# A two-block transformer kernel: the mLSTM cells' products evenly spaced, column sums four steps later, the third mixer's round reordered

## Chip, core, metric

One NeuronCore of a Trainium2 chip runs one program. The metric is device time in microseconds (us); lower is better.

## What is computed

The reference is a float32 model of two blocks on 512 positions of width 1024. The first block (Fourier and latent attention mixers, gated convolutional FFN) is not touched. The second has two layers, each a mixer, a squared-ReLU FFN and a gated embedding. The mixers, cut to what matters here:

```
# mixer_ab: two chains, 4 heads of 128, chunks of 64 positions (8 chunks)
qa, ka = l2norm(silu(conv(..))), l2norm(silu(conv(..)))     # gated delta rule, chain A
v_new = u - w @ state;  o = q_dec @ state + attn @ v_new    # per chunk
state = state * exp(g_last) + k_dec.T @ v_new
# mLSTM, chain B, per chunk
num = inter * (q @ c_st) + pmat @ v                         # numerators
den = inter * (q @ n_st) + sum(pmat)
c_st = sc * c_st + kw.T @ v;  n_st = sc * n_st + sum(kw)
out = concat(rmsnorm(oa)*silu(z), rmsnorm(num/max(|den|,..))*o_gate) @ w_out
# mixer_c: 16 heads of 64, 4 key/value heads, window 128
q, k = rope(q), rope(k)
sc = q @ k.T * 64**-0.5  (band mask);  m = max(max(sc), sink)
pr = exp(sc - m) / (sum(exp(sc - m)) + exp(sink - m));  o = pr @ v
out = o @ w_o + b_o
```

## The kernel before

Every big product goes through `linear`. It walks "weight units" of 1024 x 128 in one global stream. A unit is 8 k-tiles; for each k-tile TensorE issues three 128x128 by 128x512 matmuls (high weight by high input, high by low, low by high; L393). ScalarE and VectorE split each unit into its high and low parts (L340, L349), three units ahead. Units of one `linear` alternate between PSUM banks 0 and 1 in the mixers; ScalarE empties a bank when its unit is done. The first two units of a `linear` run interleaved.

The mixers' small products are woven between those matmuls. Each engine has a chain written as a generator, with `until(name, n)` before each piece; after every second k-tile TensorE calls `tick(pe, 2)`, which lets its chain go on to the next two clock values. So one hook stands after each six matmuls of 512 columns, four hooks and eight ticks in a unit. ScalarE and VectorE advance by eight ticks at once, ahead of their wait for that unit's end; a piece of theirs that waits for TensorE therefore holds up the emptying of the unit behind it. No planner orders anything: the numbers in `until` do. With two generators on an engine (chain and side) each gets every tick.

`mixer_ab` (`chain_ab`) weaves both chains into the 33 units of the input projection. `unit_columns` (L1809) sums squares of a head over its 128 rows by 4 products of one column; it needs ScalarE's `norm_squares` (L2037). `unit_spread` (L1818) spreads the reciprocal roots; `apply` multiplies by them. The delta rule's cells follow (L1924 to L1938), then the mLSTM's eight cells. A cell has a first part (state increments L1983, intra-chunk numerators L1989 and denominators L1991) and, for n > 0, a second part with the carried state (L1997, L1999), which waits for VectorE's state update (L2239). In the program the 128x129 and 64-column products have four heads each. `mix_out` is the output projection: its input tiles 0 to 3 come from chain A (`fin["a"]`), 4 to 7 from chain B, and are split by ScalarE (L2376) and VectorE (L2383).

`mixer_c` (`chain_c`) weaves attention into 12 units, one pair of query heads t per round of eight ticks (`begin = 33 + 8t`), the last ones into `mix_out`. A round on TensorE: `swap` (L2483, half-rotation for rope), `turn` (L2490, 8 transposes of probabilities, twice), scores (L2520, 16 rows of the trace), values (L2537, 32 rows). VectorE does rope (L2577, L2580), mask (L2589), row maximum (L2591, L2593), `divide` (L2598, L2600), the copy of bank 7 (L2606) and the low part of the result (L2648). ScalarE does exp (L2545), the copy of bank 6 (L2552), the high part (L2563), and empties the projection's banks (L2470, `put`). GpSimd does the cosine product (L2683) and the division (L2689). Bank 2 is shared by `swap` and scores, bank 3 by scores and values. At the start VectorE computes the angles in ten dependent steps (L2617 to L2625), then ScalarE two Sin (L2556, L2557).

Of the kernel before, what the change touches and what calls it, by code (L numbers as in the profile page):

```python
# [14 lines left out]
P = 128  # L15
# [353 lines left out]
def linear(c, args, x, kt, count, n, ready, free, scalar=None, vector=None, scalar2=None, vector2=None, width=None,  # L369
           group=2, fill=None, before=None, supply=None, weave=None, slots=3, tick=None, third=0):  # L370
# [4 lines left out]
    cols = lambda j: width(j) if width else n  # L375
    block = c.stage()

    @block.tensor
    def _(pe):
# [8 lines left out]
        def products(j, k):  # L388
            p = pos + j
            w = slice((p % WSLOTS) * UN + k * P, (p % WSLOTS) * UN + k * P + P)  # L390
            for z, (wt, xt) in enumerate(((c.WHI, xh), (c.WHI, xl), (c.WLO, xh))):
                for acc, lo, q in accumulator(c, p, cols(j), slots):
                    mm = pe.matmul(acc, wt[:, w], xt[:, k * xw + lo:k * xw + lo + q],  # L393
                                   start=(k == 0 and z == 0), stop=(k == kt - 1 and z == 2))
            if k == kt - 1:
                mm.then_inc(c.units_done, 1)
# [3 lines left out]
        for k in range(kt):  # L400
# [11 lines left out]
        for j in range(group, count):  # L412
# [5 lines left out]
            for k in range(first, kt):  # L418
# [1205 lines left out]
def chain_ab(c, args, xp, ready, before, fin):  # L1624
# [52 lines left out]
    clock = {"pe": 0, "act": 0, "dve": 0}  # L1677

# [143 lines left out]
    def pe_chain(pe):  # L1822
# [8 lines left out]
        for h in range(4):  # L1831
            yield from until("pe", 44 + 8 * h)
            unit_columns(pe, stat["K"], o["SQK"], h)
        for h in range(4):
            yield from until("pe", 71 + h)
# [132 lines left out]
        for n in range(NCH):  # L1968
            yield from until("pe", 200 + 3 * n)
# [23 lines left out]
            if n:  # L1993
                yield
# [6 lines left out]
        for h in range(4):  # L2001
            yield from until("pe", 226 + h)
            unit_columns(pe, b_stat, o["SQ"], h)
        for h in range(4):
            yield from until("pe", 233 + h)
            unit_spread(pe, b_stat, 7, h, 2 + h)

    def pe_side(pe):
        for h in range(4):
            yield from until("pe", 76 + 8 * h)  # L2010
            unit_columns(pe, stat["Q"], o["VB"], h)
        for h in range(4):
            yield from until("pe", 103 + h)
# [25 lines left out]
    def act_chain(act):  # L2039
# [4 lines left out]
        yield from until("act", 69)  # L2044
# [52 lines left out]
        for n in range(NCH):  # L2097
            yield from until("act", 202 + 3 * n)
# [3 lines left out]
        for h in range(4):  # L2102
            yield from until("act", 225 + h)
# [3 lines left out]
        yield from until("act", 231)  # L2107
# [3 lines left out]
    def act_side(act):  # L2111
# [4 lines left out]
        yield from until("act", 101)  # L2116
# [19 lines left out]
    def dve_chain(dve):  # L2136
        id4 = c.a(o["ID2"], CHUNK).rearrange("p (a q) -> p a q", a=1).broadcast_to([P, 4, CHUNK])
        lasts = lambda lo: c.a(o["LAST"] + lo, NCH).rearrange("p (n a) -> p n a", a=1)
        yield from until("dve", 70)
        dve.wait_ge(*stat["K"][2].at(1))  # L2140
        dve.reciprocal(root(1), root(0)).then_inc(*stat["K"][3].up())
        for h in range(4):
            yield from until("dve", 71 + h)
# [84 lines left out]
        for n in range(NCH - 1):  # L2228
            yield from until("dve", 201 + 3 * n)
# [14 lines left out]
        yield from until("dve", 226)  # L2244
# [8 lines left out]
        yield from until("dve", 231)  # L2253
# [7 lines left out]
        for h in range(4):  # L2261
            yield from until("dve", 233 + h)
# [4 lines left out]
    def dve_side(dve):  # L2267
        lasts = lambda lo: c.a(o["LAST"] + lo, NCH).rearrange("p (n a) -> p n a", a=1)
        yield from until("dve", 102)
        dve.wait_ge(*stat["Q"][2].at(1))  # L2270
        dve.reciprocal(root(3), root(2)).then_inc(*stat["Q"][3].up())
        for h in range(4):
            yield from until("dve", 103 + h)
# [83 lines left out]
def mixer_ab(c, args, squares):  # L2357
# [7 lines left out]
    with c.pair(NL) as xp:  # L2365
        xh, xl, xw = xp
        hi, lo = c.mark("act", KT), c.mark("dve", KT)
        source = lambda k: c.a(A2["OA"] + k * NL, NL) if k < 4 else c.a(A2["QB"] + (k - 4) * NL, NL)
        block = c.stage()

        @block.scalar
        def _(act):
            act.wait_ge(c.units_done, c.pos)
            for k in range(KT):
# [4 lines left out]
        def _(dve):  # L2379
            for k in range(KT):  # L2380
                dve.wait_ge(*hi.at(k + 1))
                q = slice(k * xw, k * xw + NL)
                dve.tensor_tensor(xl[:, q], source(k), xh[:, q].bitcast(F32), ALU.subtract).then_inc(*lo.up())  # L2383
        squares = mix_out(c, args, xp, lambda k: lo.at(k + 1), c.h)
# [51 lines left out]
def chain_c(c, args, xp, ready, xh, xl):  # L2436
# [55 lines left out]

    def pe_chain(pe):
# [10 lines left out]
        for t in range(9):  # L2504
            begin = 33 + 8 * t
            yield from steps.until("pe", begin)
            if t < 8:
                swap(pe, 2 + t)
            if t:
                yield from steps.until("pe", begin + 1)  # L2510
                turn(pe, 2 * t - 2)
            if t < 8:
                yield from steps.until("pe", begin + 2)
                own(pe, (2, 3), masked.at(2 * t + 1))
                own(pe, (4, 5), masked.at(2 * t + 2))
                pe.wait_ge(*roped.at(3 + t))
                for j in range(4):
                    for r in range(2):
                        q = (64 * r, 64 * r + 64)
                        mm = pe.matmul(c.bank(2 + 2 * r + j // 2, 256, (j % 2) * 256), c.a(o["Q"] + t * NL + j * P, P, *q),  # L2520
                                       c.a(o["K"] + (t // 4) * (NL + P) + j * P, 2 * WIN, *q), start=True, stop=True)
                mm.then_inc(*scores.up())
            if t:
                yield from steps.until("pe", begin + 4)
                turn(pe, 2 * t - 1)
                yield from steps.until("pe", begin + (6 if t < 7 else 4))
                own(pe, (3,), low.at(t))
                pe.wait_ge(*pt_a.at(2 * t))
                pe.wait_ge(*pt_v.at(2 * t))
                if t == 1:  # L2530
                    pe.wait_ge(*v_put.at(2))
                    pe.wait_ge(*cleared.at(3))
                for j in range(4):
                    for z in range(2):
                        for r in range(2):
                            kv = 2 * ((t - 1) // 4) + r
                            mm = pe.matmul(c.bank(3, P, j * P, 64 * r, 64 * r + 64), c.a(o["V"] + (j + z) * 256 + kv * 64, 64),  # L2537
                                           pt(r, (2 * j + z) * P, P), start=(z == 0), stop=(z == 1))
                mm.then_inc(*values.up())
# [14 lines left out]
    def act_chain(act):  # L2554
        act.wait_ge(*angle.at(10))
        act.activation(sin, tmp(1), ACT.Sin).then_inc(*wave.up())  # L2556
        act.activation(cos, s(0, NL, NL), ACT.Sin).then_inc(*wave.up())  # L2557
        for t in range(10):
            begin = 33 + 8 * t
            yield from steps.until("act", begin)  # L2560
            if t >= 2:
                act.wait_ge(*values.at(t - 1))
                act.activation(xh[:, (t - 2) * NL:(t - 1) * NL], c.bank(3), ACT.Copy).then_inc(*high.up())  # L2563
            if 1 <= t <= 8:
                exp(act, 2 * t - 1)
                copy_a(act, 2 * t - 2)
                yield from steps.until("act", begin + 3)
                copy_a(act, 2 * t - 1)
            if t < 8:
                yield from steps.until("act", begin + 4)  # L2570
                exp(act, 2 * t)
# [634 lines left out]
```

## Time and profile before

| | us |
|---|---|
| median of 3 runs | 3305.43 (3297.83 to 3309.86) |
| the profiled execution, its own time | 3311.63 |
| its span | 3309.8 |
| TensorE busy | 3179.3 |
| VectorE busy | 1560.5 |
| ScalarE busy | 1164.3 |
| GpSimd busy | 166.5 |

In the trace mixer_ab with its output projection stands at about 1800 to 2236 us and mixer_c at about 2675 to 2880 us. A matmul row counts as busy whatever the clock, so TensorE's busy time hides half-clock stretches; the granted clock (1.00 is 2.4 GHz, 0.50 is 1.2 GHz) is in a column of its own. A float32 product written once in the program makes two rows in the trace.

### The profile page before, as it was taken

How to read it: one execution, taken by the hardware profiler on the slowest of the kernel's cores; microseconds unless marked ns; L12 is line 12 of the kernel's file. 1: busy time of each engine (PE TensorE's matmuls, PEld its weight loads, DVE VectorE, ACT ScalarE, POOL GpSimd, SP SyncE). 2: the span in 40 equal slices, each digit the busy share in tenths (PEclk: the TensorE clock that was granted, in tenths of full speed). 3: DMA queues.
4: the chain of work that ended last, by engine and by line, in shares of the span. 5: the costliest groups of instructions: out<-in, count | busy, mean ns of one | idle time of the engine just before them, and what ended most of it. 6: DMA issues, size and time to landing. Idle time of an engine off the chain costs nothing.

```text
span 3309.8 us, 42475 instructions
## 1 busy us (share of the span) xinstructions
PE 3179.3 (96%) x17484; PEld 2511.5 (76%) x17484; DVE 1560.5 (47%) x2346; ACT 1164.3 (35%) x1892; POOL 166.5 (5%) x222
## 2 busy tenths in 40 slices
PE   7999999999999999999999999999999988899999
PEld 4656687888888756788887777877888767788887
DVE  3234544434445445564557453236334567453445
ACT  3134523213223334442334532234222435332233
POOL 0022200000000012000000010000000014000000
PEclk9999999999999999999998899799999999999999
DMA  7500014333212300122322111023222221222222
GB/s 278 215 1 1 7 45 159 120 132 124 64 58 77 118 2 1 52 94 97 96 96 81 54 32 44 32 70 102 90 95 96 77 75 38 76 96 96 96 96 70
DMA packets 74031, 269.28 MB, mean 81 GB/s; under 512 B 9064, under 2 KB 9832, under 8 KB 72560
## 3 DMA queue, kind: packets, MB, share of 16 engines
q1 hardware_dynamic: 73840, 266.57, 23.7%
q8 instruction: 140, 2.29, 0.3%
q14 instruction: 51, 0.42, 0.0%
HBM read 264.44 MB, written 2.10 MB: 81 GB/s over the span
## 4 chain that ended last, share of the span: by engine, by line
PE 87%; DVE 5%; issue 3%; ACT 2%; DMA 1%; POOL 1%; SPq 0%; DVEq 0%; POOLq 0%; ACTq 0%
PE PS L393 65%; PE PS L1366 4%; PE PS L1389 2%; PE PS L1376 2%; PE PS L1292 2%; PE PS L486 1%; DMA room<-in_w_ada 1%; PE PS L1346 1%; POOL room L2689 1%; PE PS L2947 1%; PE PS L570 0%; DVE room L1716 0%; PE PS L1320 0%; PE PS L1809 0%; PE PS L1818 0%
## 5 line engine op out<-in xcount | busy, mean ns | idle before, releaser
L393 PE MATMUL PS<-room,WHI 128*128 128x512 f32 (+1 forms) x7200 | 2030.9, 378 | 31.6 <-ACT room L2470 6.2
L393 PEld LDWEIGHTS PS<-room,WHI 128*128 128x128 f32 x7200 | 1264.1, 190 | 325.5 <-issue 61.4
L393 PE MATMUL PS<-room,WLO 128*128 128x512 f32 (+1 forms) x3600 | 1242.7, 375 | 0.0
L393 PEld LDWEIGHTS PS<-room,WLO 128*128 128x128 f32 x3600 | 636.1, 190 | 125.2
L349 DVE TENSOR_TENSOR WLO<-RING,WHI 128x1024 fp32r<-128x1024 f32 x371 | 455.1, 1227 | 278.8 <-ACT WHI L340 277.4
L340 ACT ACTIVATE WHI<-RING 128x1024 fp32r<-128x1024 f32 x371 | 390.3, 1054 | 557.4 <-PE PS L393 523.8
L931 DVE SCALAR_TENSOR_TENSOR H<-PS,VEC,H 128x511 f32<-128x511 f32 (+1 forms) x132 | 83.1, 657 | 307.3 <-ACT H L909 307.3
L909 ACT ACTIVATE H<-PS,VEC 128x512 f32<-128x512 f32 (+1 forms) x132 | 88.4, 704 | 348.8 <-PE PS L393 348.8
L1366 PE MATMUL PS<-room 96*128 96x256 f32 (+1 forms) x432 | 155.8, 480 | 10.4 <-DVE room L1528 8.1
L874 DVE SCALAR_TENSOR_TENSOR X<-PS,MOD,X 128x512 f32<-128x512 f32 x96 | 60.5, 658 | 217.4 <-PE PS L393 217.4
L1572 DVE TENSOR_REDUCE room<-PS 128x1 f32<-128x768 f32 (+1 forms) x120 | 101.9, 849 | 98.9 <-PE PS L1366 98.4
L1366 PEld LDWEIGHTS PS<-room 96*128 96x128 f32 x432 | 74.7, 191 | 64.7 <-issue 57.3
L2990 DVE TENSOR_TENSOR room<-PS,room 128x512 f32<-128x512 f32 x64 | 44.2, 690 | 165.8 <-ACT room L2986 107.5
L2986 ACT ACTIVATE room<-PS 128x512 f32<-128x512 f32 x64 | 38.1, 596 | 199.1 <-PE PS L393 199.1
L1592 POOL TENSOR_SCALAR room<-room 128x768 f32<-128x768 f32 (+1 forms) x60 | 49.2, 820 | 1135.6 <-DVE room L1558 1135.6
L3015 DVE TENSOR_TENSOR X<-X,PS 128x512 f32<-128x512 f32 x48 | 33.0, 687 | 134.2 <-PE PS L393 134.2
L1552 DVE COPY room<-PS 128x384 f32<-128x384 f32 (+1 forms) x120 | 59.5, 496 | 59.2 <-PE PS L1376 59.0
L936 DVE SCALAR_TENSOR_TENSOR H<-PS,VEC,H 128x511 f32<-128x511 f32 (+1 forms) x132 | 83.2, 658 | 3.1
L486 PE MATMUL PS<-room,SC 128*32 128x512 f32 x336 | 59.5, 738 | 25.9 <-DMA room<-in_w_ada 25.9
L1389 PE MATMUL PS<-room 128*64 128x128 f32 x1248 | 82.7, 280 | 1.2 <-DVE room L1552 1.2
L1389 PEld LDWEIGHTS PS<-room 128*64 128x64 f32 x1248 | 68.1, 138 | 20.5 <-issue 18.9
L1292 PE MATMUL PS<-room 128*128 128x512 f32 (+1 forms) x210 | 77.3, 514 | 0.0
(370 smaller groups left out, 2622.8 us busy)
## 6 DMA issues: line engine op xcount, KB each, us to landing
RING<-in_stream SPq DMA_DIRECT2D x370, 512.0 KB, 3.4
room<-in_w_ada SPq DMA_DIRECT2D x84, 512.0 KB, 5.7
H<-in_w_ada SPq DMA_DIRECT2D x12, 512.0 KB, 4.6
room<-in_consts SPq DMA_DIRECT2D x4, 1024.0 KB, 9.2
room<-in_wq SPq DMA_DIRECT2D x2, 1728.0 KB, 6.9
X<-in_x_in SPq DMA_DIRECT2D x2, 1536.0 KB, 10.0
room<-in_wple SPq DMA_DIRECT2D x2, 1024.0 KB, 4.9
out_dram<-H SPq DMA_DIRECT2D x8, 256.0 KB, 2.0
```

What stands on the lines that cost most here:

```text
L340: act.activation(c.WHI[:, w:w + UN], c.RING[:, r:r + UN], ACT.Copy).then_inc(c.w_hi, 1)
L349: dve.tensor_tensor(c.WLO[:, w:w + UN], c.RING[:, r:r + UN], c.WHI[:, w:w + UN].bitcast(F32), ALU.subtract).then_inc(c.w_lo, 1)
L393: mm = pe.matmul(acc, wt[:, w], xt[:, k * xw + lo:k * xw + lo + q], start=(k == 0 and z == 0), stop=(k == kt - 1 and z == 2))
L486: mm = pe.matmul(c.bank(self.bank, 512, 0, 32 * j, 32 * j + 32), c.SC[:, 32 * k:32 * k + 32], self.ring[self.slots[k]][j // 2][:, 512 * (j ...
L909: ins = act.activation(cv(i, z, lo, w), a, ACT.Identity, bias=col("b_dw", j), scale=col("dw1_", j))
L931: ins = dve.scalar_tensor_tensor(y, a[:, 0:w - 1], col("dw0_", j), y, ALU.mult, ALU.add)
L936: ins = dve.scalar_tensor_tensor(y, a[:, 1:w], col("dw2_", j), y, ALU.mult, ALU.add)
L1292: mm = pe.matmul(c.bank(b + r, m), c.a(w + k * stride, P), c.a(x + k * W + lo, m), start=(k == 0), stop=(k == kn - 1))
L1366: mm = pe.matmul(c.bank(b + r, m), q_at(p, z, i * P, P, 0, 96), k_at(p, z, k0 + lo, m, 0, 96), start=True, stop=True)
L1376: mm = pe.transpose(c.bank(4 + (k >= half), P, (k % half) * P), probs_at(a, k * P, P), c.ID[:])
L1389: mm = pe.matmul(c.bank(6 + part, P, (i % 4) * P, 64 * z, 64 * z + 64), c.a(vv + (t0 + t) * 768 + (2 * pair + z) * 64, 64), turned_at(a + ...
L1572: dve.tensor_reduce(c.a(NEG + j, 1), c.PS[:, 512 * b:512 * b + n], AX, ALU.max, negate=True).then_inc(*neg.up())
```

## The change

1. **mLSTM cells.** `cell_at(n) = 198 + 4n` (200 for n = 0) replaces `200 + 3n`. The second part comes two ticks after the first, for every cell; before, one tick, which was in the same hook for every second cell. Their followers (column sums, roots, spreads and products at the end of chain B) move 4 to 10 ticks later. Chain A's spreads at the end stay.
2. **Column sums later.** Those of K go from ticks 44 + 8h to 48 + 8h, those of Q from 76 + 8h to 80 + 8h, with roots and spreads four ticks later. ScalarE's squares and the blocks after them stay.
3. **mix_out of mixer_ab** takes input tiles 4 to 7 first, then 0 to 3; the splitting follows.
4. **mixer_c.** ScalarE's Sin and VectorE's use of it move to tick 9, after the first two units' emptying. In a round the values of head pair t-2 are taken beside `swap`; the scores of t come two k-tiles later than before, ahead of `turn(2t-2)`; `turn(2t-1)` is in the last hook. ScalarE's exp of a pair all goes into the next round, ahead of its copies; VectorE's mask is parted from its maximum (`peak`), with a copy in between; GpSimd divides pair t-1 in one go after its cosine product. No instruction is added or removed on TensorE.

```diff
-           group=2, fill=None, before=None, supply=None, weave=None, slots=3, tick=None, third=0):
+           group=2, fill=None, before=None, supply=None, weave=None, slots=3, tick=None, third=0, order=None):
+    ks = order or list(range(kt))
-        for k in range(kt):
+        for k in ks:
...
+    cell_at = lambda n: 198 + 4 * n if n else 200
...
-            yield from until("pe", 44 + 8 * h)
+            yield from until("pe", 48 + 8 * h)
             unit_columns(pe, stat["K"], o["SQK"], h)
...
-            yield from until("pe", 200 + 3 * n)
+            yield from until("pe", cell_at(n))
...
             if n:
-                yield
+                yield from until("pe", cell_at(n) + 2)
...
-            yield from until("pe", 226 + h)
+            yield from until("pe", 234 + h)
             unit_columns(pe, b_stat, o["SQ"], h)
...
-            yield from until("pe", 233 + h)
+            yield from until("pe", 243 + h)
...
-            yield from until("pe", 76 + 8 * h)
+            yield from until("pe", 80 + 8 * h)
             unit_columns(pe, stat["Q"], o["VB"], h)
...
-            yield from until("act", 202 + 3 * n)
+            yield from until("act", cell_at(n) + (3 if n else 1))
...
-            yield from until("dve", 201 + 3 * n)
+            yield from until("dve", cell_at(n) + 1)
...
+        order = [4, 5, 6, 7, 0, 1, 2, 3]
...
+            if 2 <= t < 8:
+                take_values(pe, t - 2)
+            if t < 8:
+                yield from steps.until("pe", begin + (4 if t < 7 else 1))
+                score(pe, t)
             if t:
-                yield from steps.until("pe", begin + 1)
                 turn(pe, 2 * t - 2)
...
-                yield from steps.until("pe", begin + 4)
+                yield from steps.until("pe", begin + (6 if t < 7 else 4))
                 turn(pe, 2 * t - 1)
...
+            if t >= 7:
+                take_values(pe, t - 1)
...
     def act_chain(act):
+        yield from steps.until("act", 9)
         act.wait_ge(*angle.at(10))
...
+            if 1 <= t <= 8:
+                exp(act, 2 * t - 2)
...
-            if t < 8:
-                yield from steps.until("act", begin + 4)
-                exp(act, 2 * t)
```

**Order on TensorE, the mLSTM cells.** Before, a first part with its second part, six matmuls of 512 columns (L393), and the next cell's first part:

```order
L1983 MATMUL PS<-room 128x129 x4
L1989 MATMUL PS<-room 128x64 x4
L1991 MATMUL PS<-ONES,room 64x1 x4
L1997 MATMUL PS<-X,room 128x64 x4
L1999 MATMUL PS<-room,X 64x1 x4
L393 MATMUL PS<-room,WHI 128x512 x2
L393 MATMUL PS<-room,WLO 128x512
L393 MATMUL PS<-room,WHI 128x512 x2
L393 MATMUL PS<-room,WLO 128x512
L1983 MATMUL PS<-room 128x129 x4
```

Now (lines shifted by two, L393 is L394):

```order
L1985 MATMUL PS<-room 128x129 x4
L1991 MATMUL PS<-room 128x64 x4
L1993 MATMUL PS<-ONES,room 64x1 x4
L394 MATMUL PS<-room,WHI 128x512 x2
L394 MATMUL PS<-room,WLO 128x512
L394 MATMUL PS<-room,WHI 128x512 x2
L394 MATMUL PS<-room,WLO 128x512
L1999 MATMUL PS<-X,room 128x64 x4
L2001 MATMUL PS<-room,X 64x1 x4
```

Three of the seven cells with a second part had both parts in one hook before; now every part has six matmuls of 512 columns on either side.

**Order on VectorE, one attention round.** Before, from rope to the weight split:

```order
L2577 TENSOR_TENSOR room<-PS,room 128x512
L2580 TENSOR_TENSOR room<-H,room 128x512
L2648 TENSOR_TENSOR room<-PS,room 128x512
L2606 COPY room<-PS 128x512
L2598 TENSOR_TENSOR MS<-MS 128x4
L2600 RECIPROCAL MS<-MS 128x4
L2589 SCALAR_TENSOR_TENSOR room<-PS,room 128x1024
L2591 TENSOR_REDUCE MS<-room 128x4
```

Now (L2586 and L2589 rope, L2609 and L2611 `divide`, L2662 the low part, L2598 mask, L2617 the copy, L2602 the maximum):

```order
L2586 TENSOR_TENSOR room<-PS,room 128x512
L2589 TENSOR_TENSOR room<-H,room 128x512
L2609 TENSOR_TENSOR MS<-MS 128x4
L2611 RECIPROCAL MS<-MS 128x4
L2662 TENSOR_TENSOR room<-PS,room 128x512
L2609 TENSOR_TENSOR MS<-MS 128x4
L2611 RECIPROCAL MS<-MS 128x4
L2598 SCALAR_TENSOR_TENSOR room<-PS,room 128x1024
L2617 COPY room<-PS 128x512
L2602 TENSOR_REDUCE MS<-room 128x4
```

Both divides now stand between rope and the mask, and the copies stand behind the masks.

## Rows read from the trace of the kernel before

**Rows 1.** The page, its first line and part 1.
```profile
span 3309.8 us, 42475 instructions
...
PE 3179.3 (96%) x17484; PEld 2511.5 (76%) x17484; DVE 1560.5 (47%) x2346; ACT 1164.3 (35%) x1892; POOL 166.5 (5%) x222
```

**Rows 2.** Waits of TensorE, 1825 to 2200 us: total, times, longest.
```profile
PE PS L1809 <- ACT room L2037: 9.6, 5, 3.2
PE PS L393 <- DVE room L2383: 2.3, 1, 2.3
PE PS L1818 <- DVE room L2260: 2.1, 1, 2.1
```

**Rows 3.** Timeline, 1830 to 1840 us: start, duration, instruction, idle before.
```profile
1836.91 0.61 ACT L2037 ACTIVATE room<-room 128x512 f32<-128x512 f32 x1
...
1837.67 1.84 PE L1809 MATMUL PS<-ONES,room 128*128 128x1 f32 x8 [3.15 <-ACT room L2037]
```

**Rows 4.** Busy time by engine in four stretches, then TensorE's granted clock.
```profile
1825.00:1915.00 90.00, 79.48 (x484) 61.85 (x482) 39.20 (x71) 45.02 (x81) 3.17 (x5) 0.85 0.13 45
2003.00:2050.00 47.00, 47.00 (x297) 37.97 (x295) 16.44 (x35) 8.46 (x14) 0.00 (x0) 1.00 0.11 35
2089.40:2103.00 13.60, 13.60 (x107) 11.91 (x106) 4.43 (x14) 3.21 (x5) 0.00 (x0) 1.00 0.12 40
2103.00:2151.40 48.40, 48.40 (x220) 40.97 (x218) 6.62 (x18) 3.46 (x7) 0.00 (x0) 0.54 0.07 22
```

**Rows 5.** Timeline of TensorE, 2097 to 2104 us.
```profile
2097.44 1.00 PE L1997 MATMUL PS<-X,room 128*128 128x64 f32 x8
...
2098.93 0.74 PE L393 MATMUL PS<-room,WHI 128*128 128x512 f32 x2
...
2100.53 1.16 PE L1983 MATMUL PS<-room 64*128 64x129 f32 x8
...
2103.01 1.37 PE L1997 MATMUL PS<-X,room 128*128 128x64 f32 x8
```

**Rows 6.** Groups by line and form, TensorE, 2103 to 2151.4 us.
```profile
L393 PE MATMUL PS<-room,WLO 128*128 128x512 f32 x14 | 8.8, 628 | 0.0
L1997 PE MATMUL PS<-X,room 128*128 128x64 f32 x40 | 8.0, 370 | 0.0
L1983 PE MATMUL PS<-room 64*128 64x129 f32 x32 | 7.7, 412 | 0.0
```

**Rows 7.** Waits of TensorE, 2680 to 2845 us.
```profile
PE PS L2520 <- DVE room L2648: 7.9, 5, 1.6
PE PS L393 <- ACT room L2470: 6.2, 2, 5.9
PE PS L2490 <- POOL room L2689: 3.4, 2, 3.0
PE PS L393 <- DVE room L2648: 2.9, 2, 1.4
PE PS L2520 <- DVE room L2580: 2.1, 2, 1.1
PE PS L2537 <- DVE room L2606: 1.8, 2, 0.9
PE PS L2483 <- ACT room L2470: 1.5, 1, 1.5
```

**Rows 8.** Busy time and clock, start of mixer_c and five attention rounds.
```profile
2690.00:2701.00 11.00, 8.46 (x23) 6.14 (x24) 6.68 (x10) 4.20 (x6) 3.34 (x2) 0.69 0.32 97
2745.86:2816.06 70.20, 63.63 (x453) 50.21 (x454) 50.63 (x80) 36.91 (x114) 29.92 (x45) 1.00 0.12 39
```

**Rows 9.** Timeline of ScalarE, 2690 us.
```profile
2690.76 0.63 ACT L2556 ACTIVATE room<-room 128x512 f32<-128x512 f32 x1 [5.60 <-DVE room L2625]
```

**Rows 10.** Timeline of GpSimd, 2740 us.
```profile
2740.20 2.88 POOL L2689 TENSOR_SCALAR room<-room,MS 128x256 f32<-128x256 f32 x4 [5.72 <-DVE MS L2600]
```

**Rows 11.** The page, part 5, weight splitting on VectorE.
```profile
L349 DVE TENSOR_TENSOR WLO<-RING,WHI 128x1024 fp32r<-128x1024 f32 x371 | 455.1, 1227 | 278.8 <-ACT WHI L340 277.4
```

More of the change, by code:

```diff
@@ L417, in _ @@
                 begin(j)
-            for k in range(first, kt):
+            for k in ks[first:]:
                 products(j, k)
@@ L2102, in act_chain @@
         for h in range(4):
-            yield from until("act", 225 + h)
+            yield from until("act", 231 + h)
             if h == 0:
@@ L2106, in act_chain @@
             norm_squares(act, b_stat, "QB", h, o["SQ"])
-        yield from until("act", 231)
+        yield from until("act", 237)
         act.wait_ge(*m_den.at(5))
@@ L2261, in dve_chain @@
         for h in range(4):
-            yield from until("dve", 233 + h)
+            yield from until("dve", 241 + h)
             if h == 0:
@@ L2373, in _ @@
             act.wait_ge(c.units_done, c.pos)
-            for k in range(KT):
+            for k in order:
                 act.wait_ge(*(fin["a"].at(k + 1) if k < 4 else fin["b"].at(k - 3)))
@@ L2379, in _ @@
         def _(dve):
-            for k in range(KT):
-                dve.wait_ge(*hi.at(k + 1))
+            for i, k in enumerate(order):
+                dve.wait_ge(*hi.at(i + 1))
                 q = slice(k * xw, k * xw + NL)
                 dve.tensor_tensor(xl[:, q], source(k), xh[:, q].bitcast(F32), ALU.subtract).then_inc(*lo.up())
-        squares = mix_out(c, args, xp, lambda k: lo.at(k + 1), c.h)
+        squares = mix_out(c, args, xp, lambda k: lo.at(order.index(k) + 1), c.h, order=order)
     c.high = None
@@ L2491, in turn, with score, take_values @@
         mm.then_inc(*turned.up())
+    def score(pe, t):
+        own(pe, (2, 3), masked.at(2 * t + 1))
+        own(pe, (4, 5), masked.at(2 * t + 2))
+        pe.wait_ge(*roped.at(3 + t))
+        for j in range(4):
+            for r in range(2):
+                q = (64 * r, 64 * r + 64)
+                mm = pe.matmul(c.bank(2 + 2 * r + j // 2, 256, (j % 2) * 256), c.a(o["Q"] + t * NL + j * P, P, *q),
+                               c.a(o["K"] + (t // 4) * (NL + P) + j * P, 2 * WIN, *q), start=True, stop=True)
+        mm.then_inc(*scores.up())
+    def take_values(pe, v):
+        own(pe, (3,), low.at(v + 1))
+        pe.wait_ge(*pt_a.at(2 * v + 2))
+        pe.wait_ge(*pt_v.at(2 * v + 2))
+        if v == 0:
+            pe.wait_ge(*v_put.at(2))
+            pe.wait_ge(*cleared.at(3))
+        for j in range(4):
+            for z in range(2):
+                for r in range(2):
+                    kv = 2 * (v // 4) + r
+                    mm = pe.matmul(c.bank(3, P, j * P, 64 * r, 64 * r + 64), c.a(o["V"] + (j + z) * 256 + kv * 64, 64),
+                                   pt(r, (2 * j + z) * P, P), start=(z == 0), stop=(z == 1))
+        mm.then_inc(*values.up())
     def pe_chain(pe):
@@ L2628, in dve_chain @@
         dve.memset(c.a(o["V"], 256), 0.0).then_inc(*cleared.up())
+        yield from steps.until("dve", 9)
         dve.wait_ge(*wave.at(2))
@@ L2674, in _ @@
     def _(pool):
-        for t in range(-2, 9):
-            i = t + 2
+        for i in range(11):
             if i < 10:
```

78 lines of the change are left out of this document (27 added, 51 removed).

## The prediction

> **What bounds the kernel now.** I read the page first. TensorE is busy 3179.3 of 3309.8 us [rows 1], so a gain can come from two places only: the 130 us in which TensorE stands still, and stretches in which it works at a lower clock, which its busy time doesn't show. The page's slices of granted clock dip around 2100 us, so I asked for the busy time by stretch there, then for TensorE's waits in the two mixers that the change touches, and last for the timeline around each wait.
>
> In mixer_ab, the waits between 1825 and 2200 us are led by the column sums: 9.6 us in five waits for ScalarE's squares, then 2.1 us for a reciprocal before the second chain's spreads and 2.3 us at the start of mix_out [rows 2]. Worse than these is the clock. From 2103.0 to 2151.4 us, TensorE is "busy" 48.4 of 48.4 us at a mean clock of 0.54 [rows 4], so it works at 1.2 GHz for nearly the whole stretch, without standing still once. These are the mLSTM cells. The delta rule's cells, woven with one part in each hook, kept 1.00 throughout (2003 to 2050 us) [rows 4]. In mixer_c the waits sum to 25.8 us [rows 7]: 7.9 for the low part of the values in five rounds, 5.9 once at the start, the rest at the first two rounds and the end.
>
> **The change part by part, as a sum.**
>
> *(a) Second part apart from the first.* What stands right before the fall: a second part (2097.44), six wide matmuls (2098.93), a first part (2100.53) and, at 2103.01, a second part with nothing wide between [rows 5]. From there each instruction takes longer: a product of L1997 rows 1.37 against 1.00 us for eight. Pieces at full clock, from start to start: second part 1.49, six wide matmuls 1.60, first part 2.48 us. The slow stretch holds 14 low-part matmuls, so 7 packs of six, 40 rows of L1997, so 5 second parts, and 32 rows of L1983, so 4 first parts [rows 6]. At full clock that is 5 x 1.49 + 4 x 2.48 + 7 x 1.60 = 28.6 us, against 48.4 measured: 19.8 us. The new order never joins two parts, and its densest stretch of small products is the first part alone, 2.48 us between two packs. In the 13.6 us before the fall, two first parts stood alone like this and the clock was 1.00 [rows 4]. I take the whole 19.8; the other end is zero, since nothing in the trace shows eight cells in the new spacing. The state update has time: a second part now comes two packs and a part behind the increments that it waits for.
>
> The Trainium skill ("TensorE: Matmul & The Clock Gate", section "Why this matters for your kernels") has the clock fall when TensorE stands idle between bursts of matmuls. Here it fell with no idle time at all, so the trace says more than that rule; by the rule alone spacing the parts would change nothing, which is the second case below.
>
> *(b) Sums four ticks later.* A sum now has 12 wide matmuls more ahead of it, 2 x 1.60 = 3.2 us at full clock. The longest of the five waits is 3.2 us [rows 2]: the squares start at 1836.91 and the sum at 1837.67 after 3.15 us idle [rows 3]. All five are covered, 9.6 us. For Q each square also moves ahead of the sum by a whole unit of ScalarE's queue, since the squares stay at their ticks. What is queued behind: reciprocal, spreads and `apply` move too, and ScalarE now waits for the first turned K tile one hook into the next unit before it may empty the last one. That bank isn't needed for another unit, over 5 us; I put 0.6 us against it. The mean clock over 1825 to 1915 us is 0.85 [rows 4]: 0.15 x 90 / 0.5 = 27 us at half clock. The clock falls at the four-column products before the first sum, which stay, and around the waits. I let half of the 27 us go; 3 of these 13.5 us are the first wait itself, so 10.5 us of work at half clock become 5.2. Bounds 0 and 10. Sum of (b): 9.6 - 0.6 + 5.2 = 14.2 us.
>
> *(c) End of chain B.* The spreads come ten ticks later, over a unit of wide matmuls, and the reciprocal is there: 2.1 us. The new order of input tiles in mix_out is worth nothing by itself: the first low part (L2383) stands on VectorE behind the last tile of chain A, whichever tile it makes, so the 2.3 us stay [rows 2].
>
> *(d) Start of mixer_c.* ScalarE held the finished first units back while it waited for the angles: 5.60 us, then Sin at 2690.76 [rows 9], and the emptying only behind it. Now it empties first, and the third unit starts at once. But the angles are no earlier, so Sin still ends near 2692. VectorE first splits two weight units at 1.23 us each [rows 11] and only then rotates, so the first rotation is read out at about 2695.2. TensorE reaches the second `swap`, which needs the same bank, after 18 wide matmuls (3 x 1.60) from 2686.7, so near 2691.8, and waits some 3.4 us. Of 5.9 us 2.5 go. The clock there is 0.69 over 11 us [rows 8], 6.8 us at half; half of the loss goes, 1.7. Sum 4.2 us; bounds 1 and 8.
>
> *(e) First two attention rounds.* Gone: 1.5 for a bank's emptying (exp no longer stands ahead of it), 2.1 for rope, since scores come one hook later, 0.4 of the 3.4 for GpSimd [rows 7]. Together 4.0; 3.5 after what may stay.
>
> *(f) Five full rounds.* Now 70.2 / 5 = 14.04 us each, with 7.9 us of waits in all [rows 7, 8], so 12.46 us of work. I follow a new round from its unit's start: swap and values at 1.5, scores 6.7 to 8.6, first turn to 9.4, second turn at 10.9. VectorE, after scores: mask, copy, maximum, mask, copy, maximum, split, until about 16.8, then rope until 18.1. TensorE wants the next scores at 6.7 + 12.4 = 19.1: 1 us of room. VectorE has 50.6 / 5 = 10.1 us of work in a round, GpSimd 6.0 [rows 8]; neither fills 12.4. GpSimd's division takes up to 2.88 us [rows 10] from about 18.5, so it ends by 21.4, and the first turn comes at 21.1: a wait of a few tenths at worst. I leave 0.2 us a round: 7.9 - 1.0 = 6.9 us; bounds 0 and 9.
>
> *(g) End of mixer_c.* There 8.0 us stand now: 3.0 for GpSimd, 2.9 for low parts, 1.8 for copies, 0.3 for a bank [rows 7]. The last pair still runs alone through exp, division, turn, copy, values and split; following the new queues the same way leaves 6.6. Gain 1.4.
>
> Sum: 19.8 + 14.2 + 2.1 + 4.2 + 3.5 + 6.9 + 1.4 = 52.1 us. The profiled execution took 3311.63, which gives 3259.5. It lies 6.2 us above the median of the runs, 3305.43; taken from that, 3253.3. I say **3254**.
>
> **The other ways it could go.**
>
> *The clock falls in the cells anyway.* For it: a part and its neighbour are still small products for over half the time, and the parts of the delta rule that kept 1.00 have no one-column products. Against: the fall came just at the joined parts [rows 5]. Then the 19.8 us stay: 3274. Chance 0.20.
>
> *Attention becomes bound by its helpers.* VectorE now has nearly everything between one round's scores and the next's in one string; 1 us of room is little, and if rope, GpSimd's cosine or the division come 1.5 us late, TensorE waits at the scores or the turn instead. Then (f) and part of (e) give nothing: 3254 + 9 = 3263. Chance 0.12; with the case above, 3283, 0.03.
>
> *Slower.* The half clock starts at the first cell and isn't shaken off, because packs of six don't suffice to raise it. All cells then run at the ratio of 48.4 to 28.6, 1.7: 8 first and 7 second parts with 15 packs are 19.8 + 10.4 + 24.0 = 54 us at full clock, 92 at half. The same work took 13.7 + 48.4 + about 4.6 = 67 us before: 25 us more. Should the remaining 35 us up to mix_out stay slow too, another 25. Less (b) to (g), 32.3, that is 18 us slower, 3323. It decides only if the slow clock outlasts the cells. Chance 0.03.
>
> *The change does little.* If each removed wait comes back one instruction later, as (d) partly shows, and the clock falls too, the time stays within 0.5%, which is about what a measurement of this kernel can tell from no change. Chance 0.05.
>
> **How the numbers follow.** The forecast's own case has 0.57. Faster by over 0.5% (below 3289) are it and the two next ones with their joint case, 0.92; within 0.5%, 0.05; slower 0.03. For the range: upward, the clock's case at 3274 and the joint one at 3283 go in. Downward, the high ends of (b), (d) and (f) with 0.5 us of waits gone elsewhere give 10 us or so: 3242. I say 3240 to 3284.
>
> **What the profile will show.** (a): granted clock of 1.00 across the cells, L1985 rows never followed by L1999 rows. (b): no wait of the sums for ScalarE, five before. (c): no wait for the reciprocal, still 2.3 us at mix_out's start. (d): a wait of some 3.4 us at the second `swap`, none at the third unit. (f): rounds of 12.4 to 12.8 us without a wait before scores. The prediction is wrong if the clock in the cells is below 1.00 for more than 10 us, or if rounds still take 14 us.

## The result: 39 us faster, 13 us short of the sum

The changed kernel took 3265.96 us (median of 4 runs, 3263.37 to 3275.56) against 3305.35 before (4 runs, 3297.83 to 3309.86): ratio 0.9884, 95% interval 0.9862 to 0.9906. It is faster, inside the range and 12 us above the 3254 that were forecast: it gains 39.4 us where the sum has 52.1. The execution of it that was profiled took 3275.56, so the two profiles lie 36.0 us apart (spans 3309.8 and 3273.8 us).

The page of the changed kernel, first line and part 1:

```profile
span 3273.8 us, 42474 instructions
PE 3160.7 (97%) x17484; PEld 2495.8 (76%) x17484; DVE 1560.0 (48%) x2346; ACT 1164.7 (36%) x1891; POOL 159.8 (5%) x222
```

TensorE's busy time fell by 18.6 us with the same products [rows 1]: about half of the distance between the profiles is clock, the other half waits. Its waits in the two mixers, first 1825 to 2200 us, against [rows 2]:

```profile
PE PS L394 <- DVE room L2386: 2.3, 1, 2.3
PE PS L1820 <- DVE room L2143: 2.2, 1, 2.2
PE PS L2032 <- ACT room L1732: 1.4, 1, 1.4
PE PS L1843 <- DVE H L2151: 1.0, 1, 1.0
...
PE PS L1848 <- DVE room L2158: 0.4, 1, 0.4
PE PS L1887 <- ACT room L2065: 0.3, 1, 0.3
PE PS L1811 <- ACT room L2039: 0.3, 1, 0.3
```

The 9.6 us of the column sums (L1811 now) are down to 0.3, but the first K spread (L1820) now waits 2.2 us for its reciprocal (L2143) and two steps behind it 1.4 us together. Then 2620 to 2830 us, against [rows 7]:

```profile
PE PS L2486 <- DVE room L2586: 4.9, 1, 4.9
PE PS L394 <- DVE room L2662: 2.8, 2, 1.4
PE PS L2503 <- DVE room L2589: 2.4, 1, 2.4
PE PS L2518 <- DVE room L2617: 1.7, 2, 0.9
...
PE PS L394 <- ACT room L2473: 1.4, 1, 1.4
PE PS L2493 <- POOL room L2701: 1.2, 1, 1.2
```

Low part (L394 for L2662) and copy (L2518 for L2617) of the last pair stay; the second `swap` (L2486) waits 4.9 us and the second scores (L2503) 2.4. The full rounds up to the scores at 2768.65 us have no wait; the 1.4 us for a bank stand right behind them, at 2775.35. The rows of the second `swap` and of the scores, TensorE, 2673 to 2769 us:

```profile
2673.89 1.73 PE L2486 MATMUL PS<-room,MS 128*128 128x512 f32 x2 [4.95 <-DVE room L2586]
...
2705.80 2.00 PE L2503 MATMUL PS<-room 64*128 64x256 f32 x16 [2.39 <-DVE room L2589]
...
2718.53 2.00 PE L2503 MATMUL PS<-room 64*128 64x256 f32 x16
2743.59 2.00 PE L2503 MATMUL PS<-room 64*128 64x256 f32 x16
2756.12 2.00 PE L2503 MATMUL PS<-room 64*128 64x256 f32 x16
```

From 2743.59 to 2756.12 a round takes 12.53 us; before 14.04. Stretches by clock, the kernel before and then the changed one: from the first woven product (the columns of the gates) to the delta rule's y0, from the first mLSTM cell to the last spread, and for the changed kernel the first 15 us of mix_out. The last number but two is the granted clock.

```profile
1825.71:1908.47 82.76, 73.06 (x406) 57.13 (x405) 33.76 (x61) 40.77 (x77) 1.47 (x2) 0.84 0.14 46
2089.40:2190.33 100.93, 98.83 (x547) 84.93 (x547) 26.71 (x55) 17.97 (x28) 0.00 (x0) 0.78 0.12 37
```

```profile
1831.26:1905.54 74.28, 70.39 (x398) 56.34 (x397) 33.93 (x61) 39.40 (x76) 1.48 (x2) 0.86 0.16 51
2086.64:2165.49 78.85, 78.85 (x548) 68.66 (x547) 26.69 (x55) 19.50 (x29) 0.00 (x0) 1.00 0.15 46
2168.87:2183.87 15.00, 15.00 (x59) 12.18 (x60) 6.38 (x9) 5.32 (x8) 0.00 (x0) 0.89 0.11 36
```

The cells run at 1.00 throughout, as forecast. The whole difference between the two profiles, cut at the same instructions:

| Stretch | before | after | difference | forecast |
|---|---|---|---|---|
| start to first woven product (same code) | 1825.7 | 1831.3 | +5.6 | 0 |
| to the first mLSTM cell: (b) | 263.7 | 255.4 | -8.3 | -14.2 |
| to mix_out: (a), (c) | 104.3 | 82.2 | -22.1 | -21.9 |
| to mixer_c's first product (same code but for mix_out's order) | 481.7 | 483.5 | +1.8 | 0 |
| to the second turning of V: (d) | 35.5 | 34.2 | -1.3 | -4.2 |
| to the last low part: (e), (f), (g) | 129.3 | 119.1 | -10.2 | -11.8 |
| to the end (same code) | 469.6 | 468.2 | -1.5 | 0 |

Stretches of the same code thus differ by up to 6 us between two executions. And the close fit of the cells' row, 22.1 against 21.9, is partly by construction: the forecast was read from the very execution that it is compared with here. What a part is worth has to come from experiments.

### The profile page after: what moved, and what is told of

The parts are those of the page before. It is cut to its first block, busy times and chain, and to the rows that moved or that the text cites. A ratio compares the mean times of both kernels' runs of the same rounds, so it can differ in the third digit from the quotient of the medians.

```text
span 3273.8 us, 42474 instructions
## 1 busy us (share of the span) xinstructions
PE 3160.7 (97%) x17484; PEld 2495.8 (76%) x17484; DVE 1560.0 (48%) x2346; ACT 1164.7 (36%) x1891; POOL 159.8 (5%) x222
## 4 chain that ended last, share of the span: by engine, by line
PE 90%; DVE 5%; ACT 2%; issue 1%; DMA 1%; SPq 0%; POOL 0%; DVEq 0%; POOLq 0%; ACTq 0%
PE PS L394 67%; PE PS L1367 4%; PE PS L1390 2%; PE PS L1377 2%; PE PS L1293 2%; PE PS L487 2%; DMA room<-in_w_ada 1%; PE PS L1347 1%; PE PS L2959 1%; PE PS L571 1%; PE PS L1820 0%; PE PS L1321 0%; PE PS L567 0%; PE PS L2518 0%; PE PS L2493 0%
## 5 line engine op out<-in xcount | busy, mean ns | idle before, releaser
L394 PE MATMUL PS<-room,WHI 128*128 128x512 f32 (+1 forms) x7200 | 2016.9, 376 | 29.2 <-DVE room L816 6.1
L394 PEld LDWEIGHTS PS<-room,WHI 128*128 128x128 f32 x7200 | 1258.3, 189 | 316.0 <-issue 57.7
L394 PE MATMUL PS<-room,WLO 128*128 128x512 f32 (+1 forms) x3600 | 1237.6, 374 | 0.0
L394 PEld LDWEIGHTS PS<-room,WLO 128*128 128x128 f32 x3600 | 633.3, 189 | 124.4
```

## The experiments

Eleven variants and the changed kernel once more, in three sets; each set has its own runs of the kernel before, given with their median: 3304.67 (35 runs) for the first four, 3309.69 (8) for the next four, 3307.57 (11) for the last.

**Each part alone.** First the cells: in the kernel before

```diff
-            yield from until("pe", 200 + 3 * n)
+            yield from until("pe", cell_at(n))
...
-                yield
+                yield from until("pe", cell_at(n) + 2)
```

with the ticks of ScalarE, VectorE and of chain B's end as in the change.

> The kernel before with the edits of the mLSTM cells alone: each cell's second part two weight tiles behind its first, the cells four tiles apart, and what follows them (last column sums, copies, reciprocal) later in step. Theory A (the cells' spacing alone keeps the clock up, whatever stands before): 19 to 22 us off the time before, the stretch from the first cell's first matmul to mix_out's first about 82 us instead of 104, granted clock 1.00 in it. Rival B (the clock in the cells came out well in the changed kernel because the earlier edits moved everything ahead of them by 8 us): less than 12 us off, with stretches at half clock among the cells. Rival C (the gain comes from the later column sums behind the cells and the order of mix_out's tiles, not from the cells): under 5 us off.

Second, the K and Q column sums, with square roots, reciprocals, spreads and the products behind them three or four ticks later:

```diff
-            yield from until("pe", 44 + 8 * h)
+            yield from until("pe", 48 + 8 * h)
             unit_columns(pe, stat["K"], o["SQK"], h)
...
-            yield from until("pe", 76 + 8 * h)
+            yield from until("pe", 80 + 8 * h)
             unit_columns(pe, stat["Q"], o["VB"], h)
```

> The kernel before with the edits of the K and Q column sums alone (sums, square roots, reciprocals and spreads four tiles later). Theory A (the parts are independent, and the changed kernel's stage shows what this one is worth): 8 to 9 us off, from the weave's first product to the first cell about 255 us instead of 264, with a new wait of about 2 us of the first K spread on its reciprocal. Rival B (my forecast: the wait of 9.6 us goes and no new one comes): 14 us off. Rival C (the gain in that stage is the scatter of executions): 0 to 4 us off.

Third, all that the diff changes in `chain_c`, of which the core on TensorE:

```diff
+            if 2 <= t < 8:
+                take_values(pe, t - 2)
+            if t < 8:
+                yield from steps.until("pe", begin + (4 if t < 7 else 1))
+                score(pe, t)
             if t:
-                yield from steps.until("pe", begin + 1)
                 turn(pe, 2 * t - 2)
```

> The kernel before with the edits of the third mixer alone (scores ahead of turnings, values two rounds behind, tables of sine and cosine later). Theory A (as the changed kernel's stage shows): 11 to 13 us off, full rounds of 12.5 us, one wait of about 5 us at the second swap and one of 2.4 us at the second scores. Rival B (my forecast): 16 us off, the wait at the second swap 3.4 us and none at the second scores. Rival C (the attention's shorter rounds are given back at the start of the output projection): under 6 us off.

Fourth, only the order of mix_out's contraction tiles:

```diff
+        order = [4, 5, 6, 7, 0, 1, 2, 3]
...
-            for k in range(KT):
+            for k in order:
```

> The kernel before with the order of the output projection's contraction tiles alone (chain B's tiles first). Theory A: within 1 us of the time before, because what ends last before the projection is the second chain's last tile or PE's own queue, and the first product waits for a tile of chain B either way. Rival B (the order frees the projection from waiting for the second chain): 2 us or more off. Rival C (the projection now starts with the chain that ends last, and waits for it): 1 to 4 us more.

| Kernel | us | ratio, interval | weave to y0 | cells to last spread | mixer_c |
|---|---|---|---|---|---|
| cells | 3290.39 | 0.9955, 0.994 to 0.997 | 81.6 | 78.8 | 164.6 |
| sums | 3299.63 | 0.9981, 0.9967 to 0.9995 | 72.7 | 98.0 | 164.7 |
| third mixer | 3294.59 | 0.9971, 0.9958 to 0.9984 | 83.7 | 88.7 | 153.5 |
| order | 3310.52 | 1.0014, 0.9993 to 1.0035 | 81.7 | 88.7 | 164.6 |

(mixer_c: from its first product to the last low part; 164.8 in the profile of before, 153.3 in that of the changed kernel.) The order of mix_out's tiles is worth nothing that shows, and the wait of 2.3 us is there in every trace. The third mixer's part is worth 11.3 us by its stretch and 10.1 by medians. The sums took 9 to 11 us off their stretch and 5.0 off the time; the interval of that, 2 to 11 us, takes in 9 as well. And the cells took 14.3 us (interval 10 to 20), where (a) and (c) had 21.9. By medians the three parts alone add up to 29.4 us, ten short of what they bring together.

Why the cells alone brought less stands in the rows of their stretch, for the two kernels whose cells are those of before: the third mixer's, then the order's.

```profile
2097.91:2186.59 88.68, 86.58 (x547) 74.30 (x547) 26.70 (x55) 17.97 (x28) 0.00 (x0) 0.90 0.13 42
```

```profile
2079.66:2168.35 88.69, 86.59 (x548) 74.29 (x547) 26.71 (x55) 17.98 (x28) 0.00 (x0) 0.90 0.14 42
```

The same instructions that took 100.93 us at 0.78 in the profile of before took 88.68 at 0.90 here. So what the old cells lose isn't a constant. Over the 78.84 us of the new ones, 2.1 us are the wait for chain B's reciprocal; the rest, the loss by the clock, was 7.7 us in two executions and 20.0 in one. Of these two the third mixer's took about its kernel's median time, but the order's was the fastest of its ten (3289.58).

**The changed kernel again, and with the old cells.** The first is the change as it is; the second undoes its cells (`cell_at(n)` back to `200 + 3 * n`, the second part one tick behind, and followers).

> The changed kernel once more, beside the same runs of the kernel before, for a narrower interval and a second trace. Theory A (the value of the cells' spacing hangs on how much of the cells the execution before spends at half clock, and that differs between executions; the rest is fixed): 35 to 39 us off by medians, and the same stages as in the first trace to within 1 us (first cell to mix_out 82 us, third mixer 153 us). Rival B (the stages themselves differ by several us between executions in the changed kernel too): cells' stage over 85 us in this trace.

> The changed kernel with the mLSTM cells' old spacing (second parts one weight tile behind, cells three apart, followers as before). Theory A (the clock falls in the old cells in every execution, for a part of them that differs): 10 to 22 us more than the changed kernel, 14 in the median; stage from the first cell to the last spread 88 to 101 us with granted clock 0.78 to 0.90. Rival B (my step: always 20 us). Rival C (with the stages before it shortened the cells do without the spacing): under 5 us more.

The changed kernel took 3271.31 us: 38.4 off, ratio 0.9878 (0.9855 to 0.9901). The cells (78.8) and mixer_c (153.9) repeat to 0.6 us; the stretch of the sums took 72.0 instead of 74.3. With the old cells it took 3293.28, ratio 0.9953 (0.9936 to 0.9969): 22 us more by medians, 25 by the ratios. Its windows, the same two stretches:

```profile
1828.59:1901.22 72.63, 68.79 (x398) 54.65 (x397) 33.93 (x61) 39.39 (x76) 1.48 (x2) 0.88 0.16 52
2082.30:2183.22 100.92, 98.82 (x547) 84.94 (x547) 26.71 (x55) 17.99 (x28) 0.00 (x0) 0.78 0.12 37
```

So the cells' part (with chain B's end in it) is worth 14 us alone and 22 with the other parts there, though the uncertainties of the two overlap. The mean clock of the whole program fits: 0.977 to 0.979 in all five executions of this kernel, whose times span 4 us, and 0.974 to 0.983 over 35 executions of before, whose times span 23 and are the longer the lower the clock (correlation -0.78). The old cells with the new sums lost much of the clock both times (98.0 and 100.9 us), with the old sums once in three. With five traces that is a hint and no proof; if the sums gave less time than their stretch got shorter, it would explain that too: the cells then gave back a part. Why the same instructions lose so differently is not shown.

**What in the spacing counts.** Two variants of the changed kernel. In one a cell's second part follows its first at once, the cells four ticks apart:

```diff
             if n:
-                yield from until("pe", cell_at(n) + 2)
                 pe.wait_ge(*m_state.at(n))
```

> The changed kernel with each cell's second part right behind its first in one place, cells still four weight tiles apart. Theory A (the clock in the cells hangs on how many narrow products stand in a stretch of several cells, not on the place of the second part): the stage from the first cell to the last spread stays at 79 us, the time within 3 us of the changed kernel. Rival B (a cell's two parts in one place, 12 narrow products and 8 of one column in a row, are what lowers the clock): stage over 88 us, 10 us or more above the changed kernel. Under both, the second part may wait for its state, which VectorE gets from the cell before: under 1 us in all.

In the other the cells are three ticks apart and the second parts two ticks behind, with chain B's end as it was before the change:

```diff
-            yield from until("pe", cell_at(n))
+            yield from until("pe", 200 + 3 * n)
...
-                yield from until("pe", cell_at(n) + 2)
+                yield from until("pe", 202 + 3 * n)
```

> The changed kernel with the cells three weight tiles apart as before, but each second part two tiles behind its first (every other one then stands right ahead of the next cell's first part). Theory A (density counts): the stage stays at 88 to 101 us, 10 to 22 us above the changed kernel. Rival B (a cell's own two parts apart is enough): stage 79 us plus at most 2, time within 3 us of the changed kernel.

They took 3277.76 (ratio 0.991, 0.989 to 0.993) and 3277.79 (0.9907, 0.9889 to 0.9925); by the ratios, 0.9884 and 0.9878 for the changed kernel, that is 8 to 11 us above it. The intervals still touch, so most of the weight lies on the stretches, of which there is one trace each. The cells' stretch of the first and of the second:

```profile
2077.10:2163.40 86.30, 86.30 (x547) 74.32 (x547) 26.69 (x55) 19.48 (x29) 0.00 (x0) 0.90 0.13 42
```

```profile
2082.65:2167.87 85.22, 83.12 (x548) 72.71 (x548) 26.70 (x55) 18.09 (x28) 0.00 (x0) 0.94 0.15 44
```

Neither of the pure theories holds. Over 78.84 us the clock costs 7.5 us in the first and 4.3 in the second (beside 2.1 of chain B's wait); neither variant gets back to 1.00. Against the old cells (ratio 0.9953, 0.9936 to 0.9969) both are better, clear of their intervals: wider distance helps at joined parts, and a later second part helps at the old distance. The second isn't a clean test of distance, though: three ticks apart, every other second part stands right ahead of the next cell's first (one at 2097.76 us, with the next first part at 2099.25), so small products are joined there too. And joined parts don't always cost: in the first variant the clock falls behind the first pair (0.57 from 2083.6 to 2091.0 us), but from 2109.9 us it is 1.00, through four more cells with both parts together. Its trace is also of an execution 6 us faster than its median, so the usual loss may be larger.

**The two waits that the change left.** The second `swap` of mixer_c behind the first turning of V instead of ahead of it, on VectorE likewise:

```diff
-        for i in range(2):
-            yield from steps.until("pe", 10 + 2 * i)
-            swap(pe, i)
+        yield from steps.until("pe", 10)
+        swap(pe, 0)
...
             mm.then_inc(*v_turned.up())
+            if i == 0:
+                yield from steps.until("pe", 20)
+                swap(pe, 1)
```

> The changed kernel with the second rotary swap of the third mixer eight weight tiles later, behind the first turning of the values (and its rope step on VectorE with it). Theory A (the wait of 4.95 us at that swap is for the chain of sine, sign and the first rope product, and nothing needs the swap before the scores): 5 to 6.5 us less than the changed kernel, the stage from the third mixer's first product to the second turning of the values 28 to 29 us instead of 34.2. Rival B (the wait moves to the first scores, since the second rope step and the GpSimd product behind it come later): 0 to 2 us less, a wait of 3 us or more at the first or second scores.

It took 3257.24 us, ratio 0.984 (0.9818 to 0.9862). The two swaps with the turning between them (L2530, transposes of V), TensorE's timeline:

```profile
2658.40 1.02 PE L2486 MATMUL PS<-room,MS 128*128 128x512 f32 x2
2664.75 0.60 PE L2530 MATMUL PS<-ID,room 128*128 128x128 f32 x4
2666.56 1.02 PE L2486 MATMUL PS<-room,MS 128*128 128x512 f32 x2
```

No wait, and 1.02 us at full clock where it was 1.73. From mixer_c's first product to the second turning it takes 27.3 us, where the two traces of the changed kernel have 34.2 and 34.7: 7 us less, and the wait at the second scores is the same 2.4. By medians it is 14.1 us below the changed kernel of the same set. Only the 7 us are shown to be the swap's; the rest of the profiles' distance (3.3 before the weave, 1.2 in the sums' stretch, 1.7 ahead of mixer_c and 1.7 in the rounds) lies in code that is the same, where stretches differ from one execution to the next.

Next the K spreads, on top of the change (and on VectorE `74 + h` to `76 + h`):

```diff
-            yield from until("pe", 75 + h)
+            yield from until("pe", 77 + h)
             unit_spread(pe, stat["K"], 1, h, 2 + h)
...
-            yield from until("act", 77 + 4 * h)
+            yield from until("act", 77 + 4 * h if h else 80)
```

> The changed kernel with the K spreads, the products that use them and the head-by-head work behind them up to two weight tiles later; the last column sum, the square root and the reciprocal stay. Theory A (the 2.2 us at the first spread are the time from the last sum through the square root to the reciprocal, which two tiles of 1.4 us cover): 1.5 to 2.5 us less than the changed kernel, no wait over 0.5 us at the first spread. Rival B (the head-by-head work, now closer together, waits for VectorE instead): no gain, new waits of 2 us or more in all between the spreads and the first triangular product.

3266.97 us, ratio 0.9869 (0.9849 to 0.9889). TensorE's waits from 1825 to 1900 us:

```profile
PE PS L1848 <- DVE room L2158: 1.3, 1, 1.3
PE PS L1820 <- DVE room L2143: 0.8, 1, 0.8
```

2.1 us in two waits instead of 3.6 in three, but the stretch took 72.0 us, as that of the changed kernel did in this set. Inconclusive.

Third, on top of the later swap, the second maximum behind the rope step of round 1:

```diff
                 rope(dve, 2 + t)
+            if t == 1:
+                peak(dve, 1)
...
-            if t < 8:
+            if 1 <= t < 8:
                 peak(dve, 2 * t + 1)
```

> The kernel with the second swap later, and besides in round 0 of the attention VectorE takes the second maximum behind the rope step of round 1. Theory A (the 2.4 us at the second scores are VectorE's backlog of masks, maxima and a weight split ahead of that rope step; 1.4 us of it is the maximum moved): the wait falls to under 1.1 us, 1.3 to 2.4 us less than without the move. Rival B (the exponential behind the moved maximum is late, and the turnings of round 1 wait for GpSimd instead): a new wait of 1 us or more at the turnings of round 1, no gain. Against the kernel before by medians: 46 to 52 us off.

3262.77 us, ratio 0.9864 (0.9843 to 0.9884), not below the later swap alone. The waits of 2600 to 2830 us:

```profile
PE PS L2493 <- POOL room L2707: 2.8, 2, 1.5
...
PE PS L2503 <- DVE room L2591: 0.9, 1, 0.9
```

The scores wait 0.9 us instead of 2.4, but the first turning of round 1 now waits 1.5 us for GpSimd. That is rival B: the wait moved.

Last, all three together.

> The same with the later K spreads too. Theory A (the waits at the K spreads fall from 3.6 us to 2.1 and nothing else changes): 1 to 2 us less than without them. Rival B (they only change where the clock falls, as the stage's 72 us of before suggest): within 1.5 us either way. The best version if A.

3256.14 us, ratio 0.9846 (0.9827 to 0.9865), 6.6 us below the one before it. The stretch of the sums:

```profile
1825.99:1893.52 67.53, 65.39 (x398) 52.50 (x397) 33.89 (x61) 36.67 (x72) 1.48 (x2) 0.92 0.17 54
```

5 us shorter than in the third, of which the waits account for 1.7; the rest is clock, 0.92 against 0.88, which the same spreads didn't bring in their own run (0.86). This kernel and the one with the later swap are the best of all, 51 and 52 us below before, and can't be told apart. The later swap is what both have. The third has it too; its interval overlaps with theirs, and of the 8.6 us between its profile and that of the later swap alone 6.3 lie ahead of the first woven product, in code that is the same.

## Why the prediction was right, and where it was short

(a) The step is right: joined small products pulled the clock down with TensorE busy without a gap, and apart they leave it at 1.00. "The clock falls in the cells anyway" is out. The Trainium skill ("TensorE: Matmul & The Clock Gate", section "Why this matters for your kernels") ties the loss to idle gaps; by it the spacing would do nothing, and the experiment with the cells alone decides against that for this kernel. Wrong was to take 19.8 us, the loss of one execution, as the loss of all: others with the same cells lost 7.7. With (c) in it, it is 14.3 us by medians alone and 22.0 with the sums and the third mixer, so by medians (a) itself lies between 12 and 20. That the table shows this term as good as exact is luck: it hangs on which execution was profiled.

(b) Mis-sized, 14.2 against 8.3 between the two profiles. The waits of the sums are gone as forecast, but I let all that hangs on them move by the same four ticks and put 0.6 us against it. The square root now stands behind the emptying of a unit and a SiLU on ScalarE, and the K spreads two ticks behind it: 3.9 us of waits in all where I had 0.6. The clock's share was 2.8 us (half-clock time 0.16 x 82.8 x 2 = 26.5 before, 0.14 x 74.3 x 2 = 20.8 after) where I took 5.2: that half of it goes was a choice between bounds, and a fifth went. Over the traces this stretch took 81.6 to 83.7 us with the old sums (4 traces) and 70.8 to 74.3 with the new ones and the spreads of the change (8).

(c) Right: the reciprocal's wait is gone, the order by itself is worth nothing, the 2.3 us stay. Not foreseen: behind them the changed kernel runs mix_out's first 15 us at 0.89, 1.7 us lost. That is so in all eight traces that have the new order and other cells than the old ones, and in none of the other six, with the order alone or the cells alone among them. So the order may cost 1.7 us here; no run has the change without it.

(d) The step that failed by most of its size: 4.2 against 1.3. The wait at the second `swap` is 4.95 us, not 3.4, and the half clock behind it stayed. I gave the two weight splits 1.23 us each and the sign's product nothing. VectorE and then GpSimd in the changed kernel:

```profile
2666.02 0.43 DVE L2634 TENSOR_SCALAR room<-room 128x512 f32<-128x512 f32 x1
...
2668.22 3.35 DVE L349 TENSOR_TENSOR WLO<-RING,WHI 128x1024 fp32r<-128x1024 f32 x2
2671.50 1.51 DVE L2642 TENSOR_SCALAR room<-room,VEC 128x512 f32<-128x512 f32 x1
2673.14 0.69 DVE L2586 TENSOR_TENSOR room<-PS,room 128x512 f32<-128x512 f32 x1
```

```profile
2669.12 3.60 POOL L2697 TENSOR_TENSOR H<-room 128x512 f32<-128x512 f32 x2 [707.13 <-ACT room L2567]
2690.71 1.31 POOL L2697 TENSOR_TENSOR H<-room 128x512 f32<-128x512 f32 x1 [17.98 <-ACT room L2473]
```

The splits and the sign's product took 4.8 us in a row where the sum has 2.46, while GpSimd makes its first two cosine products, each side slowed by the other; that is more than the 1.5 us missing. With the `swap` moved, the same rows are as long (3.41 and 1.53), and TensorE doesn't wait. It could have been read from the trace of before, where the same two splits, beside a cosine product of 2.03 us, are this row of VectorE's timeline:

```profile
2693.56 3.64 DVE L349 TENSOR_TENSOR WLO<-RING,WHI 128x1024 fp32r<-128x1024 f32 x2 [1.13 <-ACT WHI L340]
```

The 1.23 us were the mean over all 371 splits of the program [rows 11].

(e), (f), (g) The full rounds are as followed: 12.53 us from 2743.59 to 2756.12, no wait, 1.51 less than before where the sum has 1.38. "Attention becomes bound by its helpers" is out for them. Of (e), 2.4 us came back at the second scores, behind VectorE's masks, maxima and a split, one of its small instructions drawn out by 0.9 us beside GpSimd. Of (g), low parts (2.8), copies (1.7) and GpSimd (1.2) wait 5.7 us together where 6.6 were to be left, but TensorE now waits 1.4 us more for a bank at 2775.35. Together 10.2 of 11.8.

The rest of the gap between sum and profiles, 5.9 us, lies in the stretches that were to stay as they were. Of these the one from mix_out on is 1.8 us longer, which the lower clock at mix_out's start (c) accounts for; the other 4.1 us are code that the change leaves alone. So 16.1 us are missing: 5.9 in (b), 2.9 in (d), 1.6 in (e) to (g), 5.9 in those stretches, less 0.2 in (a) and (c). Both profiled executions were slower than their medians, the one before by 6.3 us and the one after by 9.6, so by medians 13 us are missing.

## What to carry to other kernels

A loss by the clock that one trace shows is a sample, not a constant: look at two or three executions, or at another kernel with the same stage, before it goes into a sum. In this kernel small products are best spread both within a cell and from cell to cell; how far is enough had to be tried. When a step is moved later, follow each of its consumers to the engine's queue where it ends up; the price of an instruction belongs to the place where it stands, beside the engines that work there, and not to the mean over the program; and if an instruction waits for a bank that a slow chain frees, the cheapest cure may be to ask for the bank later.

## What was unexpected of the hardware

GpSimd and VectorE hold each other up: GpSimd's product of 128x512 took 1.31 us in the later rounds and 1.80 as a mean of two beside VectorE's splits; the split took 1.68 there instead of 1.22, a `tensor_scalar` of 128x512 1.51 instead of 0.43, one of four columns 1.17 instead of 0.23 (L2604 from 2699.39 to 2700.56 us, beside a product from 2699.22 to 2700.53). The Trainium skill ("SBUF — State Buffer", section "🔬 SBUF: two separate sides") has them share one pair of ports that the first comer holds for a whole instruction, and these rows agree with that. And TensorE, busy for 98.8 of 100.9 us, ran the instructions of the old cells at 0.78 in two executions, 0.81 in a third and 0.90 in two more, with lengths of the stretch that agree to 0.01 us within each pair.
